# One layer pair on one core: the second mixer's gate columns joined to its window values, and seven low parts moved to GpSimd

## What is computed

```python
h = rms_norm_2(x, attn_norm)
z = h @ w_in
splits = np.cumsum([2 * CONV_CH, NSA_WIDTH] + [KV_WIDTH] * 6).tolist()
a_conv, q, kc_r, vc_r, ks, vs, kw, vw, g = jnp.split(z, splits, axis=-1)
...
out = gb[..., 0:1] * o_c + gb[..., 1:2] * o_s + gb[..., 2:3] * o_w
```

## Time and profile before

| | |
|---|---|
| median of 3 runs | 761.33 us (760.98 to 761.99) |
| the profiled execution | 763.28 us |
| its span, first to last instruction | 761.5 us |
| instructions | 13543 |
| moved by DMA | 146.49 MB, 192 GB/s on average |
| mean granted TensorE clock | 0.983 |

### The profile page before, as it was taken

The page is one execution under the profiler, slowest core; times in us unless marked ns, Lnnn a source line. Parts: engine busy times, 40 slices in busy tenths (PEclk is TensorE's granted clock), DMA queues, the critical chain, the costliest instruction groups (busy, mean ns, idle before and its releaser), DMA issues.

```text
span 761.5 us, 13543 instructions
## 1 busy us (share of the span) xinstructions
PE 733.8 (96%) x5867; PEld 700.5 (92%) x5867; DVE 510.4 (67%) x613; ACT 369.0 (48%) x508; POOL 80.9 (11%) x76
## 2 busy tenths in 40 slices
PE   5899999999999999999999999999899999999996
PEld 4899999999999999999999999797699999998884
DVE  4998688687575777753447879974575665656361
ACT  3444444443545545544435464586654635354341
POOL 1500111003000000000005000004000321331001
PEclk9799999999999999999999979999999999999998
DMA  8989866876605776775651651333354765664511
GB/s 344 376 282 342 271 211 207 283 284 219 222 15 174 249 238 229 237 257 176 212 174 27 196 167 56 120 103 122 101 167 153 225 204 185 203 205 155 201 48 55
DMA packets 118335, 146.49 MB, mean 192 GB/s; under 512 B 4004, under 2 KB 103556, under 8 KB 118276
## 3 DMA queue, kind: packets, MB, share of 16 engines
q1 hardware_dynamic: 116912, 143.58, 57.2%
q10 hardware_dynamic: 1364, 2.05, 0.8%
HBM read 144.57 MB, written 1.05 MB: 191 GB/s over the span
## 4 chain that ended last, share of the span: by engine, by line
PE 78%; DVE 13%; ACT 5%; issue 2%; DMA 2%; POOLq 0%; SPq 0%; DVEq 0%; ACTq 0%
PE bank L596 55%; PE bank L1090 8%; DVE w_lo L1522 6%; ACT w_hi L1129 3%; DVE mod_acc L1514 3%; PE bank L778 3%; PE bank L917 2%; DMA raw<-in_w_ada 2%; DVE wide L1791 1%; PE bank L881 1%; PE bank L883 1%; PE bank L900 1%; PE bank L656 1%; PE bank L633 1%; PE bank L861 1%
## 5 line engine op out<-in xcount | busy, mean ns | idle before, releaser
L1522 DVE TENSOR_TENSOR w_lo<-raw,w_hi 128x2048 fp32r<-128x2048 f32 x108 | 243.0, 2254 | 118.9 <-ACT w_hi L1129 118.7
L1129 ACT ACTIVATE w_hi<-raw 128x2048 fp32r<-128x2048 f32 x110 | 207.0, 1886 | 220.5 <-PE bank L596 176.9
L596 PE MATMUL bank<-act_hi,w_hi 128*128 128x256 f32 x816 | 227.9, 281 | 0.5 <-ACT act_hi L1286 0.3
L596 PE MATMUL bank<-act_lo,w_hi 128*128 128x256 f32 x816 | 225.7, 278 | 1.4 <-DVE act_lo L1813 0.7
L596 PE MATMUL bank<-act_hi,w_lo 128*128 128x256 f32 x816 | 222.1, 278 | 1.4 <-DVE w_lo L1522 1.4
L596 PEld LDWEIGHTS bank<-act_hi,w_hi 128*128 128x128 f32 x816 | 154.0, 189 | 3.6 <-issue 3.1
L596 PEld LDWEIGHTS bank<-act_lo,w_hi 128*128 128x128 f32 x816 | 153.5, 188 | 2.3 <-DVE act_lo L1813 0.9
L596 PEld LDWEIGHTS bank<-act_hi,w_lo 128*128 128x128 f32 x816 | 151.0, 188 | 1.6 <-DVE w_lo L1522 1.6
L596 PE MATMUL bank<-ffn_hi,w_hi 128*128 128x256 f32 x352 | 97.9, 278 | 0.0
L596 PE MATMUL bank<-ffn_hi,w_lo 128*128 128x256 f32 x352 | 97.3, 276 | 0.6 <-DVE w_lo L1522 0.6
L596 PE MATMUL bank<-ffn_lo,w_hi 128*128 128x256 f32 x352 | 97.2, 276 | 0.0
(11 more groups left out here) (278 smaller groups left out, 1099.2 us busy)
## 6 DMA issues: line engine op xcount, KB each, us to landing
raw<-in_w_in SPq DMA_DIRECT2D x31, 1024.0 KB, 6.6
raw<-in_w_ada SPq DMA_DIRECT2D x24, 1024.0 KB, 6.8
raw<-in_w_gate_up SPq DMA_DIRECT2D x22, 1024.0 KB, 5.1
raw<-in_w_mlp_in SPq DMA_DIRECT2D x16, 1024.0 KB, 5.4
raw<-in_w_mlp_out SPq DMA_DIRECT2D x16, 1024.0 KB, 5.2
raw<-in_w_down SPq DMA_DIRECT2D x10, 1024.0 KB, 5.0
raw<-in_w_out SPq DMA_DIRECT2D x8, 1024.0 KB, 6.7
raw<-in_w_proj_conv SPq DMA_DIRECT2D x2, 1024.0 KB, 5.4
```

The source lines that it names most:

```text
L596: i = e.matmul(dst, lhs, rhs, start=start and k == 0 and (m == 0 or second is not None) and n == 0, stop=stop and k == kt - 1 and n == 2, ...
L1129: e.activation(w_hi[slot][:, 0:kt * n_cols], raw[i % N_RAW][:, 0:kt * n_cols], ACT.Copy).then_inc(hi_split, 1)
L1522: e.tensor_tensor(w_lo[slot][:, 0:kt * n_cols], raw[i % N_RAW][:, 0:kt * n_cols], w_hi[slot][:, 0:kt * n_cols].bitcast(F32), ALU.subtract) ...
```

## The change

The gate columns lose their own product. They are loaded into a buffer `g_raw` and split beside vw's 256 columns into `vwg_hi` and `vwg_lo`, whose rows are 292 columns. The joint product takes g's place ahead of the heads and writes 292 columns for each of the two token tiles, into two PSUM banks. ScalarE takes the gates from columns 256 to 291 and then copies the values. In the head loop q1, kc, w1k0, w1k1 and q2 come one step earlier than before, step 6 has no product, and vc, w1v0 and w1v1 stay where they were. GpSimd makes the low parts of seven products more.

```diff
+            with ExitStack() as before_heads:
+                g_raw = alloc(before_heads, "g_raw", [P, CHUNK_TILES, 3 * QH])
             score = [alloc(own, f"score{i}", [P, 6 * P]) for i in range(IN_FLIGHT)]
+            with ExitStack() as before_heads:
+                vwg_hi = alloc(before_heads, "vwg_hi", [P, CHUNK_TILES, CHUNK_COLS + 3 * QH], F32R)
+                vwg_lo = alloc(before_heads, "vwg_lo", [P, CHUNK_TILES, CHUNK_COLS + 3 * QH], F32R)
...
-        in2_first = ("cu", "cv", "q0", "ks", "kw", "g")
-        in2_heads = ("vs", "vw", "q1", "kc", "w1k0", "w1k1", "q2", "vc", "w1v0", "w1v1")
+        in2_first = ("cu", "cv", "q0", "ks", "kw", "vw")
+        in2_heads = ("vs", "q1", "kc", "w1k0", "w1k1", "q2", None, "vc", "w1v0", "w1v1")
...
-        POOL_LOW = (OUT2, OUT2 + 1)
+        POOL_LOW = tuple(product_of[name] for name in ("kw", "vs", "vw", "q1", "kc", "q2", "vc")) + (OUT2, OUT2 + 1)
...
+        banks.use("vw1", *in2_free["vw"])
...
                 e.dma_start(raw_view(i), source.rearrange("(k p) c -> p k c", p=P)).then_inc(raw_landed[i % N_RAW], 16)
+                if i == product_at[VWG]:
+                    sp.wait_ge(product_done, IN2)
+                    e.dma_start(g_raw[:], in2["g"].rearrange("(k p) c -> p k c", p=P)).then_inc(g_landed, 16)
...
+                if p == VWG:
+                    wh, wl, n_cols = vwg_hi, vwg_lo, CHUNK_COLS + 3 * QH
...
-                            dst = o[:, m * n_cols:(m + 1) * n_cols]
+                            dst = o[:, m * n_cols:(m + 1) * n_cols] if second is None else (o, second)[m][:, 0:n_cols]
...
-                e.activation(w_hi[slot][:, 0:kt * n_cols], raw[i % N_RAW][:, 0:kt * n_cols],
-                             ACT.Copy).then_inc(hi_split, 1)
+                if p == VWG:
+                    act.wait_ge(g_landed, 16)
+                    e.activation(vwg_hi[:, :, 0:n_cols], raw_view(i), ACT.Copy)
+                    e.activation(vwg_hi[:, :, n_cols:], g_raw[:], ACT.Copy).then_inc(hi_split, 1)
+                else:
+                    e.activation(w_hi[slot][:, 0:kt * n_cols], raw[i % N_RAW][:, 0:kt * n_cols],
+                                 ACT.Copy).then_inc(hi_split, 1)
...
+                elif name == "vw":
+                    both = b, bank[banks.bank["vw1"]]
...
+                        t = e.activation(gate[:, tt, :], both[tt][:, CHUNK_COLS:CHUNK_COLS + 3 * QH], ACT.Sigmoid,
                                          scale=rstd_col[:, tt:tt + 1])
                     t.then_inc(gate_set, 1)
                     preload(ACT.Exp)
+                    for tt in range(TT):
+                        t = e.activation(vw_nat[:, tt, :], both[tt][:, 0:CHUNK_COLS], ACT.Copy, scale=rstd_col[:, tt:tt + 1])
+                    t.then_inc(vw_set, 1)
...
                 pool.wait_ge(hi_split, p + 1)
+                if p == VWG:
+                    e.tensor_tensor(vwg_lo[:, :, 0:n_cols], raw_view(i), vwg_hi[:, :, 0:n_cols].bitcast(F32), ALU.subtract)
+                    e.tensor_tensor(vwg_lo[:, :, n_cols:], g_raw[:], vwg_hi[:, :, n_cols:].bitcast(F32),
+                                    ALU.subtract).then_inc(lo_split_pool, 1)
+                    continue
```

More of the change, by code:

```diff
@@ L318, in build @@
         product_of = {}
-        for name in in2_first + in2_heads:
+        for name in filter(None, in2_first + in2_heads):
             if name.startswith("w1"):
@@ L327, in build @@
                 plan_product(in2[name])
+        VWG = product_of["vw"]
         OUT2 = len(product_at)
@@ L360, in build @@
         rows_landed = [sem(f"rows{i}_landed") for i in range(3)]
-        x_landed, w2_landed, stored = sem("x_landed"), sem("w2_landed"), sem("stored")
+        x_landed, w2_landed, g_landed, stored = sem("x_landed"), sem("w2_landed"), sem("g_landed"), sem("stored")
         raw_landed = [sem(f"raw_landed{i}") for i in range(N_RAW)]
@@ L491, in build @@
                     "q2": (q2_copied, 3), "ks": (ks_set, 1), "kw": (kw_set, 1), "vs": (vs_set, 1), "vw": (vw_set, 1),
-                    "g": (gate_set, 1), "kc": (cmp_scaled, 1), "vc": (cmp_scaled, 2)}
+                    "kc": (cmp_scaled, 1), "vc": (cmp_scaled, 2)}
         for name in in2_first:
@@ L510, in build @@
                     banks.use("repeated", vc_set, 2)
-            if h < len(in2_heads) and not in2_heads[h].startswith("w1"):
+            if h < len(in2_heads) and in2_heads[h] and not in2_heads[h].startswith("w1"):
                 banks.use(in2_heads[h], *in2_free[in2_heads[h]])
@@ L843, in tensor_program @@
             for name in in2_first[2:]:
-                product(product_of[name], start_bank(name), *act2, tokens_first=(name == "g"))
+                product(product_of[name], start_bank(name), *act2, tokens_first=(name == "vw"),
+                        second=start_bank("vw1") if name == "vw" else None)
                 if name == in2_first[2]:
@@ L1031, in tensor_program @@
                         cmp_output(int(stage[3:]))
-                if h < len(in2_heads):
+                if h < len(in2_heads) and in2_heads[h]:
                     name = in2_heads[h]
@@ L1036, in tensor_program @@
                     else:
-                        product(product_of[name], start_bank(name), *act2, tokens_first=name in ("vs", "vw"))
+                        product(product_of[name], start_bank(name), *act2, tokens_first=(name == "vs"))
             cmp_output(QH // 2 - 1)
@@ L1323, in evacuate @@
                     e.activation(conv_s, conv_s, ACT.Sigmoid).then_inc(conv_sigmoid, 1)
[L1324 to L1331, removed]
+                elif name == "vs":
                     act.wait_ge(product_done, p + 1)
@@ L1334, in evacuate @@
                     for tt in range(TT):
-                        t = e.activation(gate[:, tt, :], b[:, tt * 3 * QH:(tt + 1) * 3 * QH], ACT.Sigmoid,
+                        t = e.activation(vs_nat[:, tt, :], src[:, tt, :], ACT.Copy, scale=rstd_col[:, tt:tt + 1])
+                    t.then_inc(vs_set, 1)
+                elif name == "vw":
+                    both = b, bank[banks.bank["vw1"]]
+                    act.wait_ge(product_done, p + 1)
+                    act.wait_ge(rstd_col_set, 1)
+                    for tt in range(TT):
+                        t = e.activation(gate[:, tt, :], both[tt][:, CHUNK_COLS:CHUNK_COLS + 3 * QH], ACT.Sigmoid,
                                          scale=rstd_col[:, tt:tt + 1])
@@ L1358, in scalar_program @@
             for name in in2_first[1:]:
-                if name == "g":
+                if name == "vw":
                     act.wait_ge(tables_pool, Q_BASE)
```

## The result

The changed kernel takes 776.87 us (median of four runs, 776.12 to 787.44) against 761.66 us (760.98 to 763.98) for the kernel before, run beside it. The ratio is 1.0226, its 95% interval 1.0136 to 1.0317: slower, as forecast, but by 15.2 us where 7.8 were worked out, and 0.87 us beyond the upper end of the range. The 15.2 us rest on four runs a side. The profiled execution took 776.12 us, its span is 774.4 us.

A forecast was written before the change was run, and what follows sets the result against it. The prediction took TensorE's own queue to bound the second mixer. Its terms, -9.4 + 2.5 + 6.5 + 0.6 + 3.1 + 4.5 = +7.8 us, raised the median from 761.33 to 769.1, rounded 769.0, range 760.0 to 776.0.

The forecast's parts named there:

- What bounds it: Second mixer: TensorE's own queue sets the end; the gate product costs as much as a full one plus a clock fall.
- Term 1: TensorE in the second mixer: gate product and its clock fall go, vw's matmuls get 36 columns more; -9.4 us.
- Term 2: Product ks: VectorE's low(ks) waits for GpSimd's split of kw and ends at 427.6; +2.5 us.
- Term 3: Joint product: GpSimd splits vs before vw, so TensorE waits for low(vw) from 439.0 to 445.5; +6.5 us.
- Term 4: Scores of head 0: VectorE's taps, held by GpSimd's splits, make kw_T late, at 452.2; +0.6 us.
- Term 5: TensorE's clock: a low stretch follows the 6.5 us wait at the joint product; +3.1 us, bounds 0 to 5.1.
- the short one: TensorE's 3.9 us wait at ks: no clock cost at the likeliest, 4.4 us at the upper bound.
- Term 6: w1k0 in the heads: q2's split delays VectorE's taps, so the pairing of kc ends late; +4.5 us.
- The long wait that was costed: The 6.5 us wait at the joint product: 6.2 us of low clock fall on work, half lost, 3.1 us.
- Costed at nothing: VectorE's six fewer splits, the g_raw load, later weight loads, ScalarE's second hi piece, vw's second bank: no time charged.
- the heavy one: Rival: both gaps drop the clock and starved taps make kw_T late; 775 to 780 us, chance 0.18.
- The estimate by start-to-start spacing: GpSimd's 2048-column split takes 3.0 us, not 4.54; the sum would then be +3.3 us.

The follow-up runs named there:

- joint_vectore: Changed kernel with the seven added low parts, the joint product's included, back on VectorE, GpSimd keeping only w_out_2's two splits: 759.29 us, ratio 0.9946 to the kernel before.
- joint_again: The joint product with its low parts made by VectorE, the same kernel as `joint_vectore`, run once more unchanged: 759.65 us, ratio 0.9972 to the kernel before.
- order_fixed: Changed kernel with only the order of GpSimd's tuple changed, to kw, vw, vs: 773.95 us, ratio 1.0135 to the kernel before.
- after_busy2: Changed kernel with 15, 27 and 18 identity matmuls filling most of TensorE's three new waits: 771.24 us, ratio 1.0105 to the kernel before.
- the two pauses: A `joint_vectore` version with later taps and an empty fifth head step (766.09 us), TensorE held at the joint product by 12 or 20 GpSimd memsets: 770.56 and 774.78 us.
- joint_hold: `joint_vectore` with 11 identity matmuls meant for TensorE's 2.8 us wait for the compressed values: 761.69 us, ratio 1.0003 to the kernel before.
- joint_start: `joint_vectore` with 24 in place of 8 filler matmuls ahead of the first modulation sum: 760.46 us, ratio 0.9999 to the kernel before.

## Why the prediction was wrong

- **What bounds it, and Term 1** (-9.4): right in kind. In `joint_vectore` the joint product's matmuls start 0.134 us apart (0.133 forecast), and its gain is 8.3 us by `joint_again`, with the three small waits taken out.
- **Term 2** (+2.5): right. The wait for low(ks) went from 1.4 to 3.9 us, and low(ks) ended when forecast (425.65 us, with all of this profile 2.0 us early), 2.15 us after the split.
- **Term 3** (+6.5): right. The wait is 6.8 us, by the order vs before vw. `order_fixed` removes it by the order alone.
- **Term 4** (+0.6): nothing. kw_T was done at 446.04, 7.9 us ahead of the scores, since all four taps were through before q1's split began at 445.23, and the clock fall made the joint product end later.
- **Term 5** (+3.1), **the clock: the step that failed.** The prediction let one wait drop the clock, charged nothing for the short one ("for the short one I charge nothing at the likeliest"), did not ask the question at all for the wait that its own Term 6 had created, and took the 2.8 us wait for safe because it had been so in one profile. All four went with a low stretch: 1.7 at ks, 2.5 at the joint product and 2.3 at w1k0, 6.5 us in place of 3.1, and 2.9 behind L962, 9.4 in all. The long wait that was costed (2.5) was even a little cheaper than forecast. `after_busy2` gives back the first three (5.85 of 6.5 us) without touching a wait's cause, and the two pauses show it on a wait made for the purpose. That the change causes the fourth fall is not shown: `joint_again`, which has none of the three waits, fell there as well, and the kernel before has one profile only, while the mean granted clock of its runs in the three groups goes from 0.979 to 0.988. The 2.9 us are what two profiles differ by.
- **Term 6** (+4.5): right, 5.1 us, by the mechanism given: taps of 7.55 in place of 3.25 us, then the pairs. The vc split cost nothing visible among TensorE's waits.
- **Missed:** 0.8 us at L654. Head step 6 has no product now, so nothing lies between the head's work and ScalarE's squares. The prediction saw the empty step and costed it nowhere.
- **Costed at nothing:** right; no load shows among TensorE's waits. VectorE loses seven splits of 2048 columns, though, not the six that the prediction counts; it changes no term.

With Term 1 as forecast and the measured values in the other terms: -9.4 + 2.5 + 6.8 + 0 + 9.4 + 5.1 + 0.8 = 15.2 us. The profiles give 12.0 + 2.9 = 14.9, the medians 15.2. With 8.3 for Term 1 it would be 16.3; 1.1 to 1.4 us are not settled, and that the first sum meets the medians to the tenth is luck.

Of the rivals the heavy one (775 to 780) has the result, and in part for the reason it gives first, both gaps dropping the clock; its other half, a late kw_T, did not come. Part of its hit is luck: it charged 4.4 us for the short gap, which cost 1.7, and the falls at w1k0 and behind L962 that make up for this stand in no rival. Its chance of 0.18 was too low, and the range, cut at 776.0, left out most of it. The estimate by start-to-start spacing, which made a split 3.0 us, is refuted: on the path the next splits start 4.69 and 4.63 us later. The Trainium skill (Perfetto Trace Analysis, "GPSIMD Engine Instruction") distrusts the recorded duration of such an instruction; for this operation record and spacing agree (4.69 for a record of 4.73).

## What to carry to other kernels

Where a change makes TensorE wait for some 3 us or more, count the wait, and then the work behind it at half the clock: here from 1.4 us behind a wait of 3.4 to 2.5 behind one of 6.8. Count it for every such wait that the change makes, those that follow from other terms too, and for an old wait that kept the clock in one profile. The 3 us are no bound: in `order_fixed` the clock fell behind a wait of 2.3 us. A split moved to GpSimd is not moved off VectorE where VectorE does two-input operations in SBUF: its 4.6 us stand in both engines' queues, so by these runs it belongs only where VectorE has nothing of the kind to do. And a queue that walks a tuple must walk it in the order in which its results are used.

## What the runs showed of the hardware

- The clock behind the same 2.8 us wait, in the same kernel, stayed at 1.00 in one execution (`joint_vectore`) and fell in another (`joint_again`). The low stretch near 20 us lasted 6.8 us in some profiles and 10.2 in others, of the same code. The Trainium skill (TensorE: Matmul & The Clock Gate, "Part 1: The HAM clock gate (the "warmup" mystery)") calls the number of slow matmuls at a kernel's start variable from run to run. No run here shows slow ones at the very start (the clock is 1.00 in the first 10 us); what the profiles show is such variation in mid-kernel. A single profile in which a wait kept the clock is thus no evidence that it will.
- A wait need not stand ahead of a fall: in `joint_hold` and `joint_start` the clock was low from about 210 to 230 us, in code that all kernels share and in which TensorE waits for nothing longer than 0.6 us from 195 us on. In `joint_hold`:

```profile
219.00:224.00 5.00, 5.00 (x25) 5.00 (x25) 0.00 (x0) 0.00 (x0) 0.00 (x0) 0.50 0.00 0
```

  In the other twelve profiles the clock did not fall there; why it did in these two is open. Those profiled executions took 770.22 and 769.04 us, 8 to 9 above the medians of these kernels.
- Filler matmuls in a wait hold the clock (S down by 5.85 us), but filler longer than the wait stands on the path: with 24, 50 and 34 of them in place of 15, 27 and 18 the time was 778.09 in place of 771.24 us.
